# The last norm of a two-layer trunk: the 64-token tile on 128 partitions in two feature halves, and tile 0's scaling and shift on ScalarE and GpSimd

## The reference

```python
def layer_norm(x, g, b):
    x32 = x.astype(jnp.float32)
    xc = x32 - jnp.mean(x32, -1, keepdims=True)
    var = jnp.mean(xc * xc, -1, keepdims=True)
    return (xc * lax.rsqrt(var + NORM_EPS) * g + b).astype(x.dtype)

# last sublayer, h = the layer's input rows, 320 tokens x 1024 features
y = layer_norm(ALPHA * h + moe_swiglu(h, router, w1, w3, w2), ln_moe_g, ln_moe_b)
# y_prompt = the first 256 rows, y_sample = the last 64
```

## Time and profile before

| | us |
|---|---|
| median of 3 runs (lowest, highest) | 1492.17 (1491.59, 1493.68) |
| the profiled execution's own time | 1491.27 |
| its span, from the first to the last instruction | 1489.3 |
| busy in it: TensorE, VectorE, ScalarE, GpSimd | 1449.5, 1188.1, 937.6, 74.9 |
| mean granted TensorE clock (1 is full) | 0.993 |

### The profile page before, as it was taken

One profiled execution on the slowest core, in us unless ns is written; L12 is line 12 of the kernel. 1 busy time (PEld: TensorE's weight loads), 2 busy tenths in 40 slices (PEclk: granted clock), 3 DMA queues, 4 the chain that ended last, 5 costly groups with the idle time before them and its releaser, 6 DMA issues.

```text
span 1489.3 us, 28994 instructions
## 1 busy us (share of the span) xinstructions
PE 1449.5 (97%) x11160; PEld 1298.6 (87%) x11161; DVE 1188.1 (80%) x1611; ACT 937.6 (63%) x1236; POOL 74.9 (5%) x148
## 2 busy tenths in 40 slices
PE   8999998999999899999999999999999999999996
PEld 8998988999999899888788888888888888888884
DVE  6686888555445798877999998899989899898997
ACT  4563144533333596565778877688787887877873
POOL 8300000000000000000000000000000000000000
PEclk9999999999999999999999999999999999999999
DMA  9421005444444353226899999999999999999992
GB/s 282 144 86 35 4 3 156 142 142 148 156 135 146 100 167 119 84 69 249 299 385 395 409 388 398 335 405 383 370 398 339 410 378 362 398 343 410 382 357 73
DMA packets 162127, 371.71 MB, mean 250 GB/s; under 512 B 10184, under 2 KB 85872, under 8 KB 162032
## 3 DMA queue, kind: packets, MB, share of 16 engines
q1 hardware_dynamic: 159256, 361.13, 66.0%
q0 software_dynamic: 2160, 7.87, 1.9%
q10 hardware_dynamic: 616, 1.37, 0.2%
HBM read 360.63 MB, written 9.71 MB: 249 GB/s over the span
## 4 chain that ended last, share of the span: by engine, by line
PE 90%; DVE 6%; ACT 2%; issue 1%; DMA 0%; SPq 0%; DVEq 0%; ACTq 0%
PE bank L546 11%; PE bank L1218 11%; PE bank L1219 10%; PE bank L1220 10%; PE bank L548 10%; PE bank L547 10%; PE bank L1242 5%; PE bank L1244 5%; PE bank L1243 5%; PE bank L637 4%; PE bank L1227 1%; PE bank L978 1%; PE bank L753 1%; DVE wd_lo L1314 0%; PE bank L1277 0%
## 5 line engine op out<-in xcount | busy, mean ns | idle before, releaser
L2004 DVE TENSOR_TENSOR w_lo<-moe_ring,w_hi 128x1024 fp32r<-128x1024 f32 (+1 forms) x560 | 608.4, 1155 | 29.7 <-ACT w_hi L2731 29.7
L2731 ACT ACTIVATE w_hi<-moe_ring 128x1024 fp32r<-128x1024 f32 (+1 forms) x560 | 531.5, 1014 | 73.4 <-PE bank L1244 39.1
L1218 PE MATMUL bank<-w_hi,xe_hi 128*128 128x512 f32 (+1 forms) x768 | 288.2, 375 | 1.3 <-DVE w_lo L2004 1.3
L546 PE MATMUL bank<-in_hi,wd_hi 128*128 128x320 f32 x872 | 275.4, 316 | 10.8 <-DVE in_lo L1697 8.9
L1219 PE MATMUL bank<-w_hi,xe_lo 128*128 128x512 f32 (+1 forms) x768 | 285.9, 372 | 0.0
L1220 PE MATMUL bank<-w_lo,xe_hi 128*128 128x512 f32 (+1 forms) x768 | 285.4, 372 | 0.0
L1314 DVE TENSOR_TENSOR wd_lo<-arena,wd_hi 128x1024 fp32r<-128x1024 f32 x141 | 169.6, 1207 | 138.9 <-ACT wd_hi L2266 138.8
L548 PE MATMUL bank<-in_hi,wd_lo 128*128 128x320 f32 x880 | 274.8, 312 | 0.0
L547 PE MATMUL bank<-in_lo,wd_hi 128*128 128x320 f32 x872 | 271.7, 312 | 0.0
L2266 ACT ACTIVATE wd_hi<-arena 128x1024 fp32r<-128x1024 f32 (+1 forms) x140 | 145.8, 1048 | 156.8 <-PE bank L548 156.7
L546 PEld LDWEIGHTS bank<-in_hi,wd_hi 128*128 128x128 f32 x872 | 165.8, 190 | 13.8 <-issue 9.7
(11 more groups left out here) (413 smaller groups left out, 1705.0 us busy)
## 6 DMA issues: line engine op xcount, KB each, us to landing
moe_ring<-in_moe_w SPq DMA_DIRECT2D x216, 1024.0 KB, 8.6
moe_ring<-in_moe_w SPq DMA_DIRECT2D x64, 768.0 KB, 5.2
arena<-in_ffn_w SPq DMA_DIRECT2D x30, 1024.0 KB, 5.4
arena<-in_w_in_c SPq DMA_DIRECT2D x16, 1024.0 KB, 5.3
arena<-in_w_in_ab SPq DMA_DIRECT2D x12, 1024.0 KB, 5.8
arena<-in_w_out_ab SPq DMA_DIRECT2D x4, 1024.0 KB, 5.0
arena<-in_w_out_c SPq DMA_DIRECT2D x4, 1024.0 KB, 5.0
arena<-in_ffn_w SPq DMA_DIRECT2D x4, 768.0 KB, 4.3
```

Source lines behind the costliest of these rows:

```text
L546: pe.matmul(b[:, 0:T], w_[0][:, cols], x_hi, start=start, stop=False)
L1218: pe.matmul(b[:, 0:w], xe_hi[:, k, :], hi_[:, c0:c1], start=(k == 0), stop=False)
L2004: dve.tensor_tensor(w_lo[:, i % UNITS, 0:unit_words(i)], moe_unit(i), w_hi[:, i % UNITS, 0:unit_words(i)], ALU.subtract)\
L2731: act.activation(w_hi[:, i % UNITS, 0:unit_words(i)], moe_unit(i), ACT.Copy).then_inc(S("e_hi"), 1)
```

## The change

Four things change, all at the end of the program but for one load.

1. Tile 2 is laid out on all 128 partitions: partitions 0 to 63 hold features 0 to 511 of the 64 tokens, partitions 64 to 127 features 512 to 1023. Its rows come by two DMAs, the identity product becomes one (into bank 6), the two picks go to the two halves of that bank's partitions. It stands ahead of tile 0's wait for `ey` on TensorE. Its gain and shift are loaded in the same layout, four more loads (`half_gain` in a free half of `xtok`, `half_shift` over `pair`); SyncE waits for two more semaphores ahead of them.
2. A token's statistics now lie on two partitions. VectorE makes mean and mean square of each half (`half_moments`), TensorE adds the halves by two products with `ident2` (a 64 x 64 identity twice, one below the other) into bank 7, VectorE turns that into mean and minus the variance.
3. VectorE's order is new: statistics of tile 0, of tile 2, centring of tile 0, statistics of tile 1, centring of 1 and 2, final scaling of 1 and 2.
4. Tile 0's multiplication with 1/std is an ACT.Copy with a scale on ScalarE, its shift an addition on GpSimd, and ScalarE issues its store. SyncE stores tile 1 and then both halves of tile 2 behind one wait.

The diff:

```diff
--- before.py
+++ after.py
@@ -298,9 +298,15 @@
         eg = e_.take(STRIP)
         ln_gb = e_.take(2 * D).rearrange("p (a n) -> p a n", a=2)
         pick = e_.take(3 * BLK).rearrange("p (i n) -> p i n", i=3)
+        pair_at = e_.at
+        assert 2 * 3 * NE * NE + NX * NX >= 512
         pair = e_.take(2 * 3 * NE * NE).rearrange("p (a i n) -> p a i n", a=2, i=3)
         compact = e_.take(NX * NX).rearrange("p (j c) -> p j c", j=NX)
 
+        half_gain = xtok[:, 2, 512:D]
+        half_shift = arena[:, pair_at:pair_at + 512]
+
+        half_moments = sb("half_moments", [P, 2])
         dC = sb("dC", [P, RF, NCH])
         ends = sb("ends", [P, HH, NCH])
         last = sb("last", [P, 2, RPC])
@@ -1281,18 +1287,27 @@
             chosen_rows(1, E_Y[0])
             def last_rows(n):
 
+                def picked(out, rows, i, half, start):
+                    return pe.matmul(out, pick[:, i, 0:rows], ey[:, half * 512:(half + 1) * 512], start=start, stop=True, skip_group_check=i == 2)
+
                 pe.wait_ge(*at_count("y_scale", 1))
-                for i, (t0, rows) in enumerate(TILES):
-                    if i:
-                        pe.wait_ge(*at_count(f"y_in{i}", 16))
-                    for half in range(2):
-                        if i:
-                            pe.matmul((E_H1, E_H3, E_T)[i][half][0:rows, :], ident[:, 0:rows], xtok[:, i, half * 512:(half + 1) * 512],
-                                      start=True, stop=False)
-                        else:
-                            pe.wait_ge(S("e_y"), 2 * n - 1 + half)
-                        pe.matmul((E_H1, E_H3, E_T)[i][half][0:rows, :], pick[:, i, 0:rows], ey[:, half * 512:(half + 1) * 512],
-                                  start=(i == 0), stop=True).then_inc(S("y_normal"), 1)
+                pe.wait_ge(*at_count("y_in2", 32))
+                pe.matmul(E_T[0][:, :], ident[:, :], xtok[:, 2, 0:512], start=True, stop=False, skip_group_check=True)
+                for half in range(2):
+                    pe.wait_ge(S("e_y"), 2 * n - 1 + half)
+                    picked(E_H1[half][:, :], P, 0, half, True).then_inc(S("y_normal"), 1)
+                for half in range(2):
+                    mm = picked(E_T[0][64 * half:64 * half + 64, :], T_SAMPLE, 2, half, False)
+                mm.then_inc(S("y_normal"), 1)
+                pe.wait_ge(*at_count("y_in1", 16))
+                for half in range(2):
+                    pe.matmul(E_H3[half][:, :], ident[:, :], xtok[:, 1, half * 512:(half + 1) * 512], start=True, stop=False)
+                    picked(E_H3[half][:, :], P, 1, half, False).then_inc(S("y_normal"), 1)
+                pe.wait_ge(*at_count("y_halves", 1))
+                for half in range(2):
+                    mm = pe.matmul(E_T[1][64 * half:64 * half + 64, 0:2], ident2[:, :], half_moments[:, :], start=True, stop=True,
+                                   skip_group_check=True)
+                mm.then_inc(S("y_joined"), 1)
 
             expert_loops(pe, expert_block, last_rows)
 
@@ -2200,44 +2215,52 @@
 
             expert_loops(dve, expert_block, last_places)
 
...
+            def moments_of(i, h, x):
+                dve.bn_stats(moments[:, i, h, :], x).then_inc(S("y_moments"), 1)
+
+            def centred(i, cols, x, gain):
+                return dve.scalar_tensor_tensor(xtok[:, i, cols], x, mean_var[:, i, 0:1], gain, ALU.subtract, ALU.mult)
 
             dve.wait_ge(*at_count("y_in0", 16))
-            dve.wait_ge(*at_count("ln_gb_in", 64))
...
+            dve.wait_ge(*at_count("ln_gb_in", 128))
+            for h in range(2):
+                dve.wait_ge(*at_count("y_normal", h + 1))
+                cols = slice(h * 512, (h + 1) * 512)
+                link(dve.tensor_tensor(xtok[:, 0, cols], xtok[:, 0, cols], E_H1[h][:, :], ALU.add))
+                moments_of(0, h, xtok[:, 0, cols])
+            dve.wait_ge(*at_count("y_moments", 2))
+            dve.bn_aggr(mean_var[:, 0, :], moments[:, 0, :, :]).then_inc(S("y_var"), 1)
+            dve.wait_ge(*at_count("y_normal", 3))
+            moments_of(2, 0, E_T[0][:, :])
+            dve.wait_ge(*at_count("y_moments", 3))
+            link(dve.bn_aggr(half_moments[:, :], moments[:, 2, 0:1, :]))
+            dve.scalar_tensor_tensor(half_moments[:, 1:2], half_moments[:, 0:1], half_moments[:, 0:1], half_moments[:, 1:2], ALU.mult, ALU.add)\
+               .then_inc(S("y_halves"), 1)
+            dve.wait_ge(*at_count("y_var", 1))
+            centred(0, slice(0, D), xtok[:, 0, :], ln_gb[:, 0, :]).then_inc(S("y_scaled"), 1)
+            for h in range(2):
+                dve.wait_ge(*at_count("y_normal", 4 + h))
+                moments_of(1, h, E_H3[h][:, :])
+            dve.wait_ge(*at_count("y_moments", 5))
+            dve.bn_aggr(mean_var[:, 1, :], moments[:, 1, :, :]).then_inc(S("y_var"), 1)
+            dve.wait_ge(*at_count("y_joined", 1))
+            link(dve.tensor_scalar(mean_var[:, 2, :], E_T[1][:, 0:2], 0.5, None, ALU.mult))
+            dve.scalar_tensor_tensor(mean_var[:, 2, 1:2], mean_var[:, 2, 0:1], mean_var[:, 2, 0:1], mean_var[:, 2, 1:2], ALU.mult, ALU.subtract)\
+               .then_inc(S("y_var"), 1)
+            dve.wait_ge(*at_count("y_var", 2))
+            for h in range(2):
+                cols = slice(h * 512, (h + 1) * 512)
+                ins_ = centred(1, cols, E_H3[h][:, :], ln_gb[:, 0, cols])
+            ins_.then_inc(S("y_scaled"), 1)
+            dve.wait_ge(*at_count("y_var", 3))
+            centred(2, slice(0, 512), E_T[0][:, :], half_gain).then_inc(S("y_scaled"), 1)
+            dve.wait_ge(*at_count("y_std", 2))
+            dve.wait_ge(*at_count("y_scaled", 2))
+            dve.scalar_tensor_tensor(xtok[:, 1, :], xtok[:, 1, :], rstd[:, 1, 0:1], ln_gb[:, 1, :], ALU.mult, ALU.add).then_inc(S("y_done"), 1)
+            dve.wait_ge(*at_count("y_std", 3))
+            dve.wait_ge(*at_count("y_scaled", 3))
+            dve.scalar_tensor_tensor(xtok[:, 2, 0:512], xtok[:, 2, 0:512], rstd[:, 2, 0:1], half_shift, ALU.mult, ALU.add)\
+               .then_inc(S("y_done"), 1)
 
 
         @block.scalar
@@ -2816,10 +2839,16 @@
                                ACT.Copy).then_inc(S("e_rows_hi"), 1)
             expert_loops(act, expert_block, outputs)
             logs_and_exps()
...
+            for i in range(3):
                 act.wait_ge(*at_count("y_var", i + 1))
-                link(act.activation(rstd[0:n, i, 0:1], mean_var[0:n, i, 1:2], ACT.Ln, bias=eps_out[0:n, :]))
-                act.activation(rstd[0:n, i, 0:1], rstd[0:n, i, 0:1], ACT.Exp, scale=-0.5).then_inc(S("y_std"), 1)
+                link(act.activation(rstd[:, i, 0:1], mean_var[:, i, 1:2], ACT.Ln, bias=eps_out[:, :], scale=-1.0 if i == 2 else 1.0))
+                act.activation(rstd[:, i, 0:1], rstd[:, i, 0:1], ACT.Exp, scale=-0.5).then_inc(S("y_std"), 1)
+                if i == 0:
+                    act.wait_ge(*at_count("y_std", 1))
+                    act.wait_ge(*at_count("y_scaled", 1))
+                    act.activation(xtok[:, 0, :], xtok[:, 0, :], ACT.Copy, scale=rstd[:, 0, 0:1]).then_inc(S("y0_scaled"), 1)
+            act.wait_ge(*at_count("y0_done", 1))
+            act.dma_start(outs[0][0][0:P, :], xtok[:, 0, :]).then_inc(S("stored"), 16)
 
         @block.gpsimd
         def _(pool):
@@ -2933,6 +2962,9 @@
 
             pool.tensor_tensor(gate_word[:, :], ones[0:1, 0:1], ones[0:1, 0:1], ALU.mult).then_inc(S("e_gate"), 2)
             expert_loops(pool, expert_block, lambda n: None)
+            pool.wait_ge(*at_count("ln_gb_in", 128))
+            pool.wait_ge(*at_count("y0_scaled", 1))
+            pool.tensor_tensor(xtok[:, 0, :], xtok[:, 0, :], ln_gb[:, 1, :], ALU.add).then_inc(S("y0_done"), 1)
 
 
         @block.sync
@@ -3031,21 +3063,27 @@
                     load_piece(n, e, p)
                     if isinstance(n, int) and p == LN_PIECE:
                         sp.wait_ge(*at_count("y_rows_in", 64))
+                        sp.wait_ge(S("extras_known"), 1)
+                        sp.wait_ge(*at_count("x_rows_in", 48))
                         for a, name in enumerate(("ln_moe_g", "ln_moe_b")):
                             sp.dma_start(ln_gb[:, a, :], ins[name][0:1, :].to_broadcast([P, D])).then_inc(S("ln_gb_in"), 16)
+                            for h in range(2):
+                                sp.dma_start((half_gain, half_shift)[a][64 * h:64 * h + 64, :],
+                                             ins[name][0:1, h * 512:(h + 1) * 512].to_broadcast([64, 512])).then_inc(S("ln_gb_in"), 16)
 
             def output_rows(n):
                 sp.wait_ge(S("e_scattered"), 16 * (n - 1))
-                for i, (t0, m_) in enumerate(TILES):
-                    sp.dma_start(xtok[0:m_, i, :], y_rows[t0:t0 + m_, :]).then_inc(S(f"y_in{i}"), 16)
+                for i in range(2):
+                    sp.dma_start(xtok[:, i, :], y_rows[i * P:(i + 1) * P, :]).then_inc(S(f"y_in{i}"), 16)
+                for h in range(2):
```

(28 more changed lines are left out.)

14 lines of the change are left out of this document (removed).

## The result

The median of 20 runs is 1494.2 us with the change and 1491.85 without, on the same chip: ratio 1.0014, 95% interval 1.0007 to 1.002. In microseconds that is +2.35 (interval +1.0 to +3.0). It lies within the 0.2% that the prediction called no change, but the interval excludes one. The forecast was 1491.7, and 1494.2 is the upper edge of its range.

A forecast was written before the change was run, and what follows sets the result against it. TensorE bounds the experts, VectorE most of the 20.60 us tail, where the change acts. VectorE's -1.17 us became -0.65 with the stores, -0.5 after a 0.15 charge: 1490.8 profiled, plus 0.9, 1491.7; range 1489.8 to 1494.2.

The forecast's parts named there:

- The stall: TensorE's tail: seven instructions fit between two code waits, so tile 0's first matmul starts at 1472.82, not 1469.61.
- Rivals 2 and 4: TensorE's tail: 2, code packet asked for 0.55 us earlier, -1.1 us, 12%; 4, TensorE starts 2.5 us earlier, 4%.
- TensorE behind it: After the stall: pairs at 0.43 us, small tile whole at 1476.7, tile 1 at 1480.20; TensorE gains little.
- VectorE: VectorE's tail chain: last instruction ends at 1485.40 instead of 1486.57, net -1.17 us.
- The list that begins "In words": VectorE's tail: operations removed against 0.9 us tiny instructions, 0.43 wait and 0.41 later start added, given as net -1.17 us.
- the sum by cadences: VectorE's tail: operation times summed in order from 1473.96, putting the end of the last instruction at 1485.40.
- The durations: Tile 0 off VectorE: ScalarE's scaling takes 1062 ns, GpSimd's 1024-wide addition is taken as 2.3 us.
- The stores: Final stores: both small-tile halves wait for one signal, span ends at 1488.6, -0.65 us; 0.15 charged for tile 1's store.
- GpSimd against VectorE: Tail: GpSimd's addition, 1480.5 to 1482.8, might block VectorE's L2248 at 1481.3; the forecast itself charged no wait.
- rival 1: Tail: VectorE's L2248 waits for GpSimd's addition to end, +1.5 us, +1.0 in all against before, 1493.1; chance 28%.
- The loads: First expert: four small loads, 0.5 MB or 1.3 us of DMA, costed at nothing because TensorE did not wait.
- Rival 3: First expert: the small loads stall TensorE, +0.5 us, 1492.7; chance 6%.

The follow-up runs named there:

- e4: The change plus eight unexecuted fp32 matmuls moving the code behind the branch 32 instructions on; 1491.21 us against 1492.24 before.
- e5: The kernel before plus eight unexecuted fp32 matmuls moving the code behind the branch 32 instructions on; 1489.88 us against 1491.72 before.
- e10: The change plus 64 unexecuted fp32 matmuls, 256 instructions or one whole code block; one run, 1495.05 us.
- e1: The kernel before plus only the four small loads and the two waits; 1492.55 us against 1492.24 before, ratio 1.0004.
- e2: The change with the four small loads issued behind the reads of y_rows at the end; 1493.48 us against 1492.24 before.
- e7: The change with the small tile's identity product behind tile 0's halves on TensorE; 1492.44 us against 1491.72 before.
- e3: The change with the small tile's variance joined from PSUM and one SBUF operand, one tiny instruction more; 1491.68 us against 1492.24 before.
- e6: The change with tile 0's scaling and shift back on VectorE, ScalarE still issuing its store; 1492.55 us against 1491.72 before.
- e11: The change with each of the four small loads issued twice; 1497.95 us against 1491.68 before, ratio 1.0039.
- e8: The change with late small loads, the variance join from PSUM and the 32-instruction code pad together; 1487.97 us against 1491.72 before.
- e9: The change with late loads, PSUM join, 32-instruction pad, and the small tile's second half stored by ScalarE; 1488.48 us against 1491.68 before.

## Why the prediction was wrong, step by step

- **The stall: right.** Seven instructions, the same restart (R + 4.23 for 4.26), tile 0 whole behind it. Rivals 2 and 4 did not happen. That the end of a block of code is the cause is now shown (e4, e5, e10) and not only inferred. That the restart differs by 0.57 us between before and e1, with the same old code around it, I had not known; it is as much as most terms of the sum. Only part of it is the packet, which comes at about R + 1.6 in before and R + 1.3 in e1; the rest lies between the packet and the restart.
- **TensorE behind it: wrong in one term.** I charged the small tile's four 64-column pairs one after the other, to 1476.7. The two that go to the two halves of the bank's partitions run at the same time: eight matmuls take 2.88 us in e2, which at 0.43 to 0.48 is six slots, and in e7 the small tile's four alone take 1.08 us, two slots. TensorEngine Tiling (Array Packing) of the Trainium skill (Key Properties) says that different tiles of the array can work in parallel, and this trace agrees; I had priced them by the old code's 64-column rows, which all went to one half. The 0.43 us that VectorE was to wait before tile 1's second statistics is not there in e2 (two statistics in 1.29 without a gap).
- **VectorE: right in the instructions, too small in the gain.** Taking the held time and the fall of the clock out, VectorE's end is 1.85 us nearer to R than in the old code: in after +0.46 = 1.04 held + 1.28 of clock - 1.86; in e2 against e1 +0.24 = 2.02 + 0.07 later restart - 1.85. I had -1.17; the missing 0.43 of wait is most of the difference. The list that begins "In words" does not add up to -1.17: its own figures give -1.79. It leaves out 1.33 us (tile 0's first addition and statistics, which ran under the stall before and now stand behind it) and counts what is removed 0.7 too small; the sum by cadences has both right.
- **The durations: right.** The addition took 2.337 us for the 2.3 taken, ScalarE's scaling 1.15 for 1.06.
- **The stores: right.** From VectorE's end to the end of the span I had 1488.75 - 1485.40 = 3.35 us; it was 3.42 (before 2.69).
- **GpSimd against VectorE: the first failed step.** I wrote that "0.8 us decide whether they meet" and took, at 47% against 28%, the case in which they don't. There was no such case: the addition was to run 1480.5 to 1482.8 and L2248 to start at 1481.3 by my own sum, inside it. The forecast put the wait at nothing, and the 47% rested on there being no row, not on a reason. The runs show 2.02 us held at full clock (e2) and 1.04 in after. SBUF — State Buffer of the Trainium skill (Who interferes with whom) says that the later of the two is blocked to the end of the other; e2, e3 and e6 agree, to 0.02 us (1482.60 and 1482.58). The price given to rival 1, +1.0 for the whole tail, is e2's tail less e1's: 21.14 - 20.14 = 1.0. That is luck: it had 1.5 us held, not 2.02, and a VectorE gain of 1.17, not 1.85, and the two errors cancel.
- **The loads: the second failed step.** "I cost it at nothing" took the wait of 0.0 before L1218 for a reserve. It says that nothing was late, not by how much. The seven traces with the four loads in have an expert stage of +0.14 to +2.05 us, 1.1 in the mean; the medians agree as far as they can (after +2.35, e2, without the early loads, +1.24, on two chips). The 1.3 us of DMA were too small as well, since the queue slowed down. Rival 3 had 6% and +0.5.
- **The clock: not foreseen.** In after TensorE fell to 1.2 GHz in the tail and VectorE reached L2248 1.28 us later. The net price is only 0.3, since 0.98 less of the held time remains: the two costs overlap. In e3, where nothing was held, it is 0.96. The fall appears in three traces (after, e3, e10) of the seven that have the change and the stall, and not in e2, e6, e7 or e11, nor in e4, e8 and e9, which have no stall. So it seems that part of the executions pay it.

The sum by the measured terms: -1.85 VectorE + 0.73 stores + 2.0 held = +0.9 in the tail, +0.3 for the clock where it falls, +1.1 in the experts: +2.0 to +2.3, against +2.35 (+1.0 to +3.0). The forecast treated the two mechanisms as rivals of which one might happen. They are independent, one in the tail and one in the experts, and had to be added. The upper end of the range, which the result just meets, was not earned either: it was to be rival 1 with an addition of 3 us, which by the forecast's rule (each us beyond 1481.3 costs one) gives 1493.9, and the addition took 2.34. What stays open is why the same loads cost TensorE 0.14 us in e10 and 2.05 in e1, when the queue lost the same in both; what makes it slow down; and what puts the restart at 3.7 or at 4.2. The cost of the clock (0.3 to 1.0) is worked out from differences of single traces, and no run changed the clock alone.

## What to carry to other kernels

When work moves to GpSimd, look for every VectorE instruction beside it that takes both inputs from SBUF, even one of a single column: here such a one was held until GpSimd was done (2.24 us for 0.22), and one operand from PSUM avoided that. A wait of 0.0 behind a full DMA queue is not slack; put small loads behind the last one that the bottleneck waits for, as e2 did at no cost. And where a profile shows "issue" on TensorE at a fixed count of instructions behind a branch, try a pad before rewriting the work: here it alone gave the old kernel 0.11% (0.02 to 0.2%).

## What the runs showed of the hardware

- Two 64-column fp32 matmuls with the same moving width, to the lower and the upper half of a bank's partitions, overlap: tile 0's four pairs and the small tile's four took 2.88 us in e2, six slots and not eight, and the small tile's four alone 1.08 us in e7.
- VectorE's L2248, one column of 128 partitions from SBUF, took 1.26 (after), 1.49 (e7), 1.97 (e10), 2.23 (e4) and 2.24 us (e2, e11) beside one GpSimd addition of 2.34 us and 0.22 without it (e6), the more the sooner behind the addition's start it came. Three centrings with one input from PSUM beside it were not held when the join wasn't (2.06 for x3 in e3 and e8, 2.05 alone in e2).
- At the edge of a block of code seven instructions behind a branch out of a loop TensorE stood for 1.2 (e1, e7) to 2.2 us (after). Moving the code by 32 instructions removed the wait (e4, e5, e8, e9); with 256 it was there (e10).
- Four loads of 128 KB in a full queue, 1.3 us of DMA by their size, cost up to 2.05 us of TensorE; eight cost 4.8. The queue moved 277 GB/s for 409 in the 5 us from 795 (after, before), with its engines as busy.
